# A two-block transformer forward pass: rope rows collected and turned inside the last quarter of the first projection, and w_ada units shared in turn between TensorE and VectorE

## The reference, cut to what matters

```
mod  = silu(c) @ w_ada + b_ada            # 2048 x 12288: 24 column blocks of 512
h    = rms_norm(x) * (1 + scale_a) + shift_a
proj = h @ w_in                            # 2048 x 5456: d_q d_k d_v s_q s_k s_v i_q i_k i_w
rope on d_q, d_k, i_q, i_k: the first 16 of each head's 64 rows
rope on s_q, s_k:           the first 32 of each head's 128 rows
score = sum_h i_w[h] * relu(i_q[h] . i_k)  # the indexer, 16 heads; then top 64 keys
8 differential heads and 8 sparse heads, softmax and values
x = x + gate_a * rms_norm(mixed @ w_o)     # then the first feed-forward
```

## Time and profile before

| | us |
|---|---|
| median of the three runs | 2827.96 |
| the profiled execution | 2830.93 |
| its span (first to last instruction) | 2829.1 |
| TensorE busy | 2626.5 (93%) |
| VectorE busy | 1399.1 (49%) |
| ScalarE busy | 1043.2 (37%) |
| GpSimd busy | 296.6 (10%) |

### The profile page before, as it was taken

How to read it: one execution, slowest core, us unless ns; L and a number is a source line. 1 busy time by engine, 2 the same in 40 slices (tenths; PEclk the granted TensorE clock), 3 DMA queues, 4 the chain that set the end, 5 groups by cost and what they waited for, 6 DMA issues and landing times. The chain is left out here.

```text
span 2829.1 us, 48216 instructions
## 1 busy us (share of the span) xinstructions
PE 2626.5 (93%) x20124; PEld 2402.9 (85%) x20124; DVE 1399.1 (49%) x1817; ACT 1043.2 (37%) x1327; POOL 296.6 (10%) x372
## 2 busy tenths in 40 slices
PE   5999989969999999999879979798899999999998
PEld 3888836959999999999869947358899999999998
DVE  2455565946674444344353354524455555554443
ACT  3533224334334343333233325323244444443332
POOL 4000043230000000012122000101200000000000
PEclk8999999989999999999989979778999999999999
DMA  7777765836785555555535411003455555554553
GB/s 280 263 248 274 272 238 196 316 108 215 244 289 193 179 183 188 167 191 178 174 87 178 148 38 60 30 1 117 136 175 178 182 180 181 187 178 160 182 185 111
DMA packets 260590, 501.56 MB, mean 177 GB/s; under 512 B 16160, under 2 KB 23035, under 8 KB 260219
## 3 DMA queue, kind: packets, MB, share of 16 engines
q1 hardware_dynamic: 249888, 492.99, 52.0%
q10 hardware_dynamic: 10603, 7.18, 0.9%
HBM read 498.05 MB, written 2.10 MB: 177 GB/s over the span
## 5 line engine op out<-in xcount | busy, mean ns | idle before, releaser
L1153 DVE TENSOR_TENSOR w_lo<-raw,w_hi 128x2048 fp32r<-128x2048 f32 (+2 forms) x386 | 862.6, 2235 | 1077.1 <-ACT w_hi L753 1077.1
L1692 PE MATMUL bank<-x_hi,w_hi 128*128 128x256 f32 (+3 forms) x4608 | 1313.8, 285 | 51.8 <-DVE w_lo L1153 17.8
L1693 PE MATMUL bank<-x_lo,w_hi 128*128 128x256 f32 (+3 forms) x4608 | 1308.7, 284 | 0.0
L1694 PE MATMUL bank<-x_hi,w_lo 128*128 128x256 f32 (+3 forms) x4608 | 1308.4, 284 | 0.0
L753 ACT ACTIVATE w_hi<-raw 128x2048 fp32r<-128x2048 f32 (+2 forms) x386 | 719.1, 1864 | 1075.5 <-PE bank L1694 945.1
L1692 PEld LDWEIGHTS bank<-x_hi,w_hi 128*128 128x128 f32 (+1 forms) x4608 | 875.5, 190 | 87.9 <-issue 37.7
L1694 PEld LDWEIGHTS bank<-x_hi,w_lo 128*128 128x128 f32 (+1 forms) x4608 | 876.5, 190 | 0.0
L1693 PEld LDWEIGHTS bank<-x_lo,w_hi 128*128 128x128 f32 (+1 forms) x4608 | 872.9, 189 | 0.0
L1692 PE MATMUL bank<-hid_hi,w_hi 128*128 128x256 f32 x1408 | 400.0, 284 | 7.9 <-POOL hid_lo L648 6.6
L1693 PE MATMUL bank<-hid_lo,w_hi 128*128 128x256 f32 x1408 | 399.1, 283 | 0.0
L1694 PE MATMUL bank<-hid_hi,w_lo 128*128 128x256 f32 x1408 | 399.0, 283 | 0.0
(11 more groups left out here) (261 smaller groups left out, 1553.2 us busy)
## 6 DMA issues: line engine op xcount, KB each, us to landing
raw<-in_w_ada SPq DMA_DIRECT2D x88, 1024.0 KB, 5.2
raw<-in_w_gate SPq DMA_DIRECT2D x88, 1024.0 KB, 5.2
raw<-in_w_up SPq DMA_DIRECT2D x88, 1024.0 KB, 5.2
raw<-in_w_in SPq DMA_DIRECT2D x68, 1024.0 KB, 5.7
raw<-in_w_down SPq DMA_DIRECT2D x64, 1024.0 KB, 5.0
raw<-in_w_down SPq DMA_DIRECT2D x32, 768.0 KB, 4.4
raw<-in_w_o SPq DMA_DIRECT2D x16, 1024.0 KB, 6.0
raw<-in_w_out SPq DMA_DIRECT2D x16, 1024.0 KB, 5.1
```

The costliest lines, as they stand in the source:

```text
L1153: dve.tensor_tensor(w_lo[ps][:, 0:width], raw[slot][:, 0:width], w_hi[ps][:, 0:width], ALU.subtract).then_inc(raw_free[slot], 1)
L1692: pe.matmul(out, wh[:, k, c], hi(k0 + k), start=a0, stop=False)
L1693: pe.matmul(out, wh[:, k, c], lo(k0 + k), start=False, stop=False)
L1694: ins = pe.matmul(out, wl_[:, k, c], hi(k0 + k), start=False, stop=z)
```

## The change

Three things are edited together.

1. **w_ada units.** SyncE's sequence of w_in and w_ada units stays as it is, but the w_ada units in the projection now belong to two sets in turn. Those behind the blocks n = 0, 2, 4, 6 go to TensorE as before. Those behind n = 1, 3, 5, 7 go to VectorE (`ada_beside`, into a buffer of its own), and TensorE adds up the partitions after block 8.
2. **Rope.** The rope stage is gone. In the last part ScalarE starts small transfers within SBUF that collect only the rows to be turned (`gather`, into `rows_iq`, `rows_sq`, `rows_d`, `rows_x`), GpSimd multiplies them by sine and cosine, TensorE swaps halves (`rotate_rows`), VectorE adds (`add_rows`) and ScalarE sends the rows back (`scatter`). There are five groups: four are turned on TensorE in the last part (after its blocks 5, 6, 8 and 10), the fifth after the value tiles. There are 30 transfers to collect and 33 back; 16 of those back start in the index stage, one behind each relu.
3. **Sets that stood in the rope stage.** The index stage keeps two sets; the heads now have four sets (two quarters in each of two heads, then columns), and the output projection four (its last block of columns had none).

```diff
-ADA_IN1, ADA_HEADS, ADA_OUT1, ADA_MLP1 = 2, 10, 17, 20
+ADA_IN1, ADA_INDEX, ADA_HEADS, ADA_OUT1, ADA_MLP1 = 2, 10, 12, 16, 20
...
-                        ada(n % 4, ADA_ORDER[ADA_IN1 + 2 * part + n // 4] * COLS)
+                        ada(n // 2, ADA_ORDER[ADA_IN1 + 2 * part + n % 2] * COLS)
...
-            rotate_cos("one", projected1)
+            for r, (src, sin, cos, _, _, _) in enumerate(turns1):
+                pool.wait_ge(rows_in[r], 16 * (2, 8, 4, 8, 8)[r])
+                if r >= 2:
+                    pool.wait_ge(r_sum, r - 1)
+                    pool.wait_ge(r_out, r - 1)
+                pool.tensor_tensor(rope_at(rope_s, r, src), src, sin, ALU.mult).then_inc(r_sin, 1)
+                pool.tensor_tensor(rope_at(rope_c, r, src), src, cos, ALU.mult).then_inc(r_cos, 1)
...
+            def gather(r, rows, tiles, dst):
+                for j in range(4):
+                    for g in range(32 // rows):
+                        act.dma_start(dst[32 * j + rows * g:32 * j + rows * g + rows, :, :],
+                                      proj[64 * g:64 * g + rows, tiles + j:tiles + 8:4, :]).then_inc(rows_in[r], 16)
...
+                elif n == 8:
+                    gather(3, 16, T_DQ, rows_d[:, 0:2, :])
+                elif n == 9:
+                    scatter(1, 16, T_IQ, rows_iq)
+                elif n == 10:
+                    scatter(2, 32, T_SQ, rows_sq)
+                    gather(4, 16, T_DK, rows_d[:, 2:4, :])
...
+                if part == 3:
+                    rope_rows(n)
...
+                if h < 8:
+                    scatter(3, 16, T_DQ, rows_d[:, 0:2, :], h)
+                else:
+                    scatter(4, 16, T_DK, rows_d[:, 2:4, :], h - 8)
...
+            def ada_beside(s, q):
+                at_ = ada_unit_at(s, q)
...
+                dve.wait_ge(raw_loaded[at_ % RAW], 16 * (at_ // RAW + 1))
+                for k in range(4):
+                    w = raw[at_ % RAW][:, k * COLS:(k + 1) * COLS]
+                    c_ = csilu[:, 4 * q + k:4 * q + k + 1]
+                    if q == 0 and k == 0:
+                        ins = dve.tensor_scalar(acc_beside[:, :], w, c_, None, ALU.mult)
+                    else:
+                        ins = dve.scalar_tensor_tensor(acc_beside[:, :], w, c_, acc_beside[:, :], ALU.mult, ALU.add)
+                    if k < 3:
+                        chain(ins)
+                ins.then_inc(raw_free[at_ % RAW], 1)
...
+                if n in (1, 3, 5, 7):
+                    ada_beside(ADA_IN1 + 2 * part + 1, n // 2)
...
+                if part == 3 and n in (6, 7, 9):
+                    add_rows({6: 0, 7: 1, 9: 2}[n])
+            add_rows(3)
...
-                if n in (4, 8):
-                    ada_columns(ADA_IN1 + 2 * part + (n == 8))
-                if n < 8:
-                    ada_quarter(ADA_IN1 + 2 * part + n // 4, n % 4)
+                if n == 7:
+                    ada_columns(ADA_IN1 + 2 * part)
+                if n in (0, 2, 4, 6):
+                    ada_quarter(ADA_IN1 + 2 * part, n // 2)
+                if n == 8:
...
+                    ins.then_inc(ada_cols, 1)
+                if part == 3 and n in (5, 6, 8, 10):
+                    rotate_rows({5: 0, 6: 1, 8: 2, 10: 3}[n])
...
-            rotate("one")
...
+            pe.wait_ge(rows_back[2], 16 * 4)
+            for r in (3, 4):
+                pe.wait_ge(rows_back[r], 16 * 8)
             heads(0, 16)
```

More of the change, by code:

```diff
@@ L153, in in1_width, with rows_before @@
     return PROJ1 - 10 * COLS if ORDER_IN1[n] == 10 else COLS
+def rows_before(s):
+    return s - min(max((s - ADA_IN1) // 2, 0), 4)
 def ada_unit_at(s, q):
[L158 to L161, removed]
+    if s >= ADA_INDEX:
+        return UNIT_INDEX + 4 * (s - ADA_INDEX) + q
+    part, half = divmod(s - ADA_IN1, 2)
+    return in1_unit(part, 2 * q + half) + 1
 TWO = [(0, 0, P), (0, P, 3 * P)]
@@ L336, in program @@
         gain_ready = sem("gain_ready")
+        rows_in = [sem(f"rope_rows_in{r}") for r in range(5)]
+        rows_back = [sem(f"rope_rows_back{r}") for r in range(5)]
         lam_summed, lam_exp = sem("lam_summed"), sem("lam_exp")
@@ L557, in _ @@
             loop(3, 8, lambda i: out1(i, unit("w_o", K_O[0], (i + 1) * COLS)))
-            for q in range(1, 4):
-                load(*unit("w_o", K_O[q], 3 * COLS))
-            load(*unit("w_gate", K16[0], 0))
+            out1(3, unit("w_gate", K16[0], 0))
             def mlp(gate, up, i, ahead, ada_block=None):
@@ L883, in _, with scatter @@
             split(UK * in1_width(0))
+            def gather(r, rows, tiles, dst):
[3 more added lines that the diff above has]
+                                      proj[64 * g:64 * g + rows, tiles + j:tiles + 8:4, :]).then_inc(rows_in[r], 16)
+            def scatter(r, rows, tiles, src, one=None):
+                act.wait_ge(r_out, r + 1)
+                for j in range(4):
+                    for g in range(32 // rows):
+                        if one not in (None, j * (32 // rows) + g):
+                            continue
+                        act.dma_start(proj[64 * g:64 * g + rows, tiles + j:tiles + 8:4, :],
+                                      src[32 * j + rows * g:32 * j + rows * g + rows, :, :]).then_inc(rows_back[r], 16)
@@ L1821, in quarters, with rotate_rows @@
                 return ready
+            def rotate_rows(r):
+                src, _, _, rot, _, dst = turns1[r]
+                pe.wait_ge(r_sin, r + 1)
+                if r >= 2:
+                    pe.wait_ge(r_out, r - 1)
+                flat = rope_at(rope_s, r, src)
+                flat = flat.rearrange("p t n -> p (t n)") if len(flat.shape) == 3 else flat
+                pe.matmul(bank[4 + r % 2][0:dst.shape[0], 0:int(np.prod(dst.shape[1:]))], rot, flat, start=True,
+                          stop=True).then_inc(r_sum, 1)
             ada_quarter(1, 0)
@@ L2000, in _ @@
             out1(0, diff_normed)
-            loop(2, (4, 4, 8), lambda i: out1(i + 1))
-            dense(K_O, FOUR, *xs(S), S)
+            loop(3, (4, 4, 8), lambda i: out1(i + 1))
             sums("attn_post")
```

166 lines of the change are left out of this document (99 added, 67 removed).

## The result

The changed kernel took 2846.39 us (median of five runs, 2843.42 to 2852.46) against 2830.72 us for the kernel before (2826.64 to 2838.83): a ratio of 1.006, 95% interval 1.0037 to 1.0083. A second set of runs of the same kernel gave 1.0061 (1.0043 to 1.008). It is 16 to 17 us slower where the forecast said no change, and its time lies above both ranges of the forecast (to 2833 and to 2841 us).

What follows compares the result with a forecast made beforehand. TensorE, busy 93% of the span, was taken as the bound, setting the projection's pace. Terms: 19.2 - 30.3 + 0.5 + 2.7 + 5.4 + 1.3 = -1.2 us, forecast 2827 us, range 2822 to 2833 (wider: 2813 to 2841).

Steps and rivals of the forecast that it cites:

- Projection, +19.2 predicted: Projection: parts 2 to 4 each 6.5 us longer from stalls for late weight units, part 1 -0.3 us; sum +19.2 us.
- a loop of takes, operations, transfers and splits: Projection, parts 2 to 4: VectorE frees slots late, giving a loop of 16.5 us for two blocks; TensorE waits 4.0 us.
- 7.80: Projection: time from SyncE starting two transfers until the second reaches ScalarE, taken as 7.80 us for 2.1 MB.
- Signs of the loop: Projection, parts 2 to 4: the profile would show TensorE waiting 3 to 4 us for `w_lo` ahead of blocks 4, 6, 8.
- Rival B: Projection: VectorE's w_ada units cost 3.6 us and more; 0.8 us more in twelve passes gives 2836.6 us; chance 0.20.
- Part 1 of it: Projection, part 1: takes are ScalarE's, the loop is 15.2 us, loss and gain nearly cancel: -0.3 us.
- Low clock after a wait: Projection: new stalls of 3 to 4 us may lower TensorE's clock; priced at nothing, since slower blocks shorten the next wait.
- Rope stage, -30.3 predicted: Rope stage of 33.0 us goes, leaving two rotations and an addition; value tiles cover the fifth group's collection: -30.3 us.
- Rival C: Behind the projection: fifth group or last scattered row late, 3 us each, ScalarE's starts delay splits; 2833 to 2838; chance 0.12.
- Index stage with its wait, +3.2 predicted: Index stage: sixteen transfer starts between relus +0.5 us; heads waiting for the last rows +2.7 us.
- 2.2 us to landing, measured on an idle queue: End of index stage: last transfer back lands 2.2 us after its start; with the start, +2.7 us (0 to 6).
- The rule weighed in the prediction: Projection transfers: fixed 2.0 us plus bytes over 436 GB/s makes the pair 6.8 us, the sum -13 us; not adopted.

Runs made afterwards that it cites:

- after: First profile of the changed kernel, nothing else edited: profiled execution 2852.46 us, the slowest of its five; span 2850.7 us.
- a2: The changed kernel run once more, nothing edited: 2848.44 us, ratio 1.0061 to the kernel before; profile span 2843.1 us.
- e2: Changed kernel with all w_ada units of the projection back on TensorE, rope change kept: 2827.5 us, ratio 0.9991 to the kernel before.
- e8: e5 with VectorE's four w_ada operations moved from behind the takes to ahead of the next block's split: 2802.62 us, ratio 0.9897.
- e11: e5 with VectorE doing only the first of four operations on each w_ada unit: 2816.95 us, ratio 0.9932.
- e5: Changed kernel with fourth group's rows sent back right behind the projection, fifth turned behind the second index head, returned behind relus 3 to 10: 2838.12 us.
- e10: Changed kernel with one added matmul of constants in TensorE's wait ahead of the fifth rotation: 2844.84 us, ratio 1.0034.
- e4: Changed kernel with only the earlier sending back of fourth and fifth groups' rows; fifth rotation stays ahead of the index stage: 2842.0 us, ratio 1.0027.
- e7: e5 plus the constant matmuls of e1 in the projection's waits: 2837.4 us, ratio 1.0012.
- e3: Kernel before with only the alternation of the projection's w_ada units between TensorE and VectorE; rope stage stays: 2859.87 us, ratio 1.0105.
- e1: Changed kernel with TensorE's waits in the projection filled by matmuls of constants: 2841.45 us, ratio 1.0033.

## Why the prediction was wrong

Step by step, with the changed kernel's two profiles (after, a2):

- **Projection, +19.2 predicted, +30.5 and +25.2 measured.** The mechanism is right (e2, e8, e11): VectorE frees the slot late, and a loop of takes, operations, transfers and splits sets the pace. The mis-sized term is "7.80" for the pair of transfers. That row was one of 23 such pairs in the trace of before (SyncE's start of the w_ada load to the start of `w_hi`), which run from 7.66 to 8.95 us with a mean of 8.15.
- **How far the loop was off.** In the nine passes of parts 2 to 4, the pair that starts when VectorE has ended its operations behind block 1, 3 or 5 takes 7.84 to 9.17 us in after, mean 8.46; the mean is 8.21 in a2 and 8.29 in e5, and the other pair now starts 3.1 to 5.5 us behind it. So 0.4 to 0.7 us more in nine passes are 4 to 6 us, of which the mean before, 8.15, would have given 3. Parts 2 to 4 have 8.2 us (after), 2.7 (a2) and 6.3 (e5) more than was priced. The passes from the `w_lo` of block 4 to those of blocks 6 and 8 take 17.4 us on average in after, 16.9 in a2 and 17.0 in e5, where 16.5 was forecast; after and e5 also take 1 to 2 us more than a2 from the `w_lo` of block 8 to that of block 10, in parts 2 and 3. Why the same code scatters so isn't settled.
- **Signs of the loop.** The waits of TensorE are as forecast ahead of blocks 4 and 6 (2.9 to 4.4 us), but not ahead of block 8 (1.2 and 2.4 us, in part 4 none). Rival B had this size and place of a loss, but named VectorE's operations, which cost what was forecast in all passes but one, where GpSimd multiplied beside them: 0.7 us. Rows with and without GpSimd were both at hand.
- **Part 1 of it, -0.3 predicted**: +2.8 and +3.0 in after and a2, +3.4 in e10, but -0.2 in e5 and -0.4 in e4, whose projections are the same code. Which one comes is left open.
- **Low clock after a wait, priced at nothing in the loop**: right there (e7), but the step stopped at the loop. The wait that mattered stood ahead of the index stage, where no later wait absorbs a slower matmul. Rule for reading: ask of every new wait what follows it, also of one of a microsecond.
- **Rope stage, -30.3 predicted**, -29.3 and -29.8 measured. The failed part is "12 starts of transfers at 0.3 to 0.4 us" and the cover by the value tiles: eight starts took 5.76 us, the rows had landed (and GpSimd began) 5.4 us after the last block instead of about 3, and the fifth group was 1.33 us late. Rival C had this, at up to 3 us; it didn't see that the clock would fall behind it.
- **Index stage with its wait, +3.2 predicted, +12.8 and +12.2 measured: 9 to 9.6 us, the largest failed step in a2 and the second in after (there the projection's is 11.3), and the one that does not scatter.** Low clock: 4.6 us (e10 against a2), a term that wasn't in the sum. Late rows: a wait of 6.8 to 7.0 us instead of 1.05, thus 5.8 where 2.7 was put (e4 has 1.16). The "2.2 us to landing, measured on an idle queue" was 6.1 us beside the ring's 1 MB loads; the forecast's own upper bound of 6 was the better number, and the row it rested on was from another state of the queues. Most of the last 2 us is the wait for a w_ada unit that e10 shows.
- **Heads +5.4, output projection +1.3**: +4.5 and +3.7, +2.0 and +1.4. Right.
- The two kernels' first dense matmuls lie 1.1 us apart (52.2 and 53.3); e3, e5 and e1 have 50.9 to 52.0. Scatter.

For a2: 6.0 + 0.5 + 9.0 - 1.7 + 0.1 + 1.1 = 15.0 us of miss, and -1.2 + 15.0 = 13.8 us against 13.9 measured at the feed-forward's first matmul.

The rule weighed in the prediction fell by the same rows: no such pair of 1 MB loads took less than 7.66 us before, or less than 7.70 us in the two profiles of the changed kernel. The Trainium skill ("DMA: Bandwidth & Descriptors", Anatomy of one DMA) has a fixed part and a rate for transfers that GpSimd starts; the estimate by it was 6.8 us. The traces disagree, for these loads started by SyncE: the mean of 8.15 us before is 1.3 us more, those of 8.21 to 8.46 us behind the change are 1.4 to 1.7 us more.

## What to carry to other kernels

When an operation frees a slot, its place in its engine's order is worth more than its duration: e5 and e8 differ in the place of four operations alone, and their projections by 33 us. Against the kernel before, the alternation costs 20 to 30 us with the operations behind the takes and gains 12 us with them in the idle time ahead of the next split. In a loop that closes over a transfer, take the mean of all its rows, with the traffic that the change will put beside it, and not the row at hand. And follow each new wait to the next stage that has no slack: there even a microsecond can cost five.

## What the runs showed of the hardware

Behind the short transposes of the value stage, waits of 1.33, 1.33 and 1.15 us (after, a2, e4) were followed by 14 to 17 us at the lower clock although TensorE was busy without a gap in them, and waits of 1.07 and 1.11 us (e1, e2) and 0.31 us (e10) were not. The falls inside the projection, behind waits of 0.8 to 4.4 us (after, a2), lasted for 11 to 27 matmul records at 0.213 us, and one wait of 3.38 us had none behind it. How long the clock stays down differs by stage, in stretches in which TensorE has no wait in either. Starting a transfer of 16 or 32 rows within SBUF occupied ScalarE's queue for 0.59 us alone and 5.76 us for eight in a row, 0.72 us each on average. Such a transfer landed 2.0 us after its issue with no 1 MB load in flight and 5.8 to 6.2 us after it beside three or four of them (after, index stage). A multiplication and addition of VectorE with two inputs in SBUF took 1.11 us beside one of GpSimd's multiplications and 0.75 us without (after; the same in a2 and e5).
